# A block's opening: x loaded and turned first, half of the conditioning weights multiplied on TensorE

## The chip, the core and the metric

The kernel runs on one core of one Trainium2 chip. The metric is the device time of one execution in microseconds, and shorter is better. A core has five engines with queues of their own: TensorE (PE, matmuls and transposes; its weight loads are shown apart as PEld), VectorE (DVE), ScalarE (ACT), GpSimd (POOL) and SyncE (SP), which here only issues transfers. They wait for one another through semaphores. PE reads SBUF and writes PSUM, which has eight banks of 512 float32 per partition.

## The reference, cut to what matters

One decoder block: a conditioning vector `c` gives six vectors of 1024 numbers (`mod`), two of which scale and shift the normalised input before the big input projection.

```python
c_act = jax.nn.silu(c)                                        # (1, 1024)
mod = (c_act @ ada_w[l] + ada_b[l]).reshape(B, N_MOD, D)      # ada_w (1024, 6144)
shift1, scale1, gate1, shift2, scale2, gate2 = [...]
h = rms_norm(x, norm1_g[l]) * (1.0 + scale1) + shift1         # x (1024, 1024)
u = h @ w_in[l]
... gated linear attention, differential attention, merge, gate1
... rms_norm with shift2, scale2, a mixture of 32 experts, gate2
```

All inputs are float32. The block goes on from `u` through two attention branches and a mixture-of-experts layer. The change touches only the way to `h`, and the first use of `h`.

## The kernel before

All is written by hand for each engine, in one block per engine, and each block runs in its written order. There is no scheduler. The opening works on:

- `aw`, four buffers of 128 x 2048 for `ada_w`. Its 1024 rows are taken as 128 partitions x 8 rows (`KT` = 8), its 6144 columns as three groups of 2048. Group 0 holds shift1 and scale1. One load (`load_ada`, L332) brings one row per partition of one group, 1 MB. The loads of group 0 from j = 4 on wait until the buffer's former content has been used (`ada_done`).
- `ada(g, j)` on DVE (L1346): `acc[:, g, :] += aw[j] * c_act[j]` per partition, one instruction of 128 x 2048. After eight of them the sum over the partitions is still to be made. PE does it for group 0 with 16 matmuls against a column of ones (L632, moving size 1), whose results are 16 columns of PSUM bank 1: S1 and, after one more DVE instruction, A1 (`mod1_done`).
- `x_all`, 8 tiles of 128 tokens x 1024, in two loads of 2 MB (`load_x`, L348). ACT squares and sums each tile and takes a square root for each four; DVE takes the reciprocal and scales the four tiles (`normalise`, L1342). PE turns each tile with 8 transposes of 128 x 128 (L650) into two PSUM banks; a pair of banks serves every other tile.
- `hT`, the turned and modulated input, 128 x 8 x 1024. DVE reads the lower bank of a tile with four instructions `bank * A1 + S1` (`modulate`, L1343), ACT the upper bank with four (L1079). So no tile leaves PSUM before A1 and S1 are there.
- `project(n)` on PE: 8 token tiles x 8 matmuls of 128 x 512 for one 512-column section of `w_in`. Three sections run first, in a loop. `wring` holds two sections of weights, 2 MB each.

SP issues all loads in one row, and a wait there holds everything behind it. POOL fills constants and clears `acc` first (L478), which the load of `ada_b` into `acc` waits for.

Of the kernel before, what the change touches and what calls it, by code (L numbers as in the profile page):

```python
# [6 lines left out]
ALU = mybir.AluOpType  # L7
ACT = mybir.ActivationFunctionType
# [7 lines left out]
P = 128  # L16
T = 1024
D = 1024
NT = T // P
KT = D // P  # L20
# [11 lines left out]
LAMBDA_INIT = 0.8 - 0.6 * float(np.exp(-0.3 * 0))  # L32
# [49 lines left out]
PI = 3.14159  # L82

SEMS = """
c_ld early_ld small_ld fills_done consts_done mask0 ada_ld0 ada_ld1 ada_ld2 ada_ld3 ada_done
cact_1 rows_tr rows_cols mod1_ps mod1_done rope_step rope_arg rope_sin
lam_done
x_ld0 x_ld1 x_sq x_sd x_rs x_norm x_tr h_evd h_eva
w_ld proj_mm proj_free
# [17 lines left out]
N_SMALL = 15  # L107


def build(nc, io, out):  # L110

    with ExitStack() as ctx:
# [16 lines left out]
        def bank(b, n=1):  # L129
            return PS[:, b:b + n, :].rearrange("p b n -> p (b n)")  # L130
# [16 lines left out]
        onesf = sb("onesf", [P, P])  # L147
# [3 lines left out]
        gcols = sb("gcols", [P, 20])  # L151
# [6 lines left out]
        cact = sb("cact", [P, 4, KT])  # L158
        S1 = sb("S1", [P, KT])
        A1 = sb("A1", [P, KT])  # L160
# [137 lines left out]
        x_v = io["x"].rearrange("(t p) n -> t p n", p=P)  # L298
# [21 lines left out]
        def _(sp_):  # L320
            e = sp_
# [5 lines left out]

            def load_ada(g, j, dynamic):

                if dynamic or g * KT + j >= 4:  # L330
                    e.wait_ge(s["ada_done"], g * KT + j - 3)
                e.dma_start(aw[j % 4], ada_v[:, j, ds(g * 2048, 2048)]).then_inc(ada_ld[j % 4], 16)  # L332

            e.dma_start(cact[:, 0, :], io["c"].rearrange("(p j) -> p j", j=KT)).then_inc(s["c_ld"], 16)
            load_ada(0, 0, False)
            load_ada(0, 1, False)
            e.wait_ge(s["fills_done"], 1)
            small(rows[0:8, :], io["norm1_g"].rearrange("(k p) -> k p", p=P), "early_ld")
            for r, nm in ((16, "diff_q_g"), (17, "diff_k_g")):
# [7 lines left out]
            def load_x(g):  # L347
                e.dma_start(x_all[:, 4 * g:4 * g + 4, :],  # L348
                            x_v[4 * g:4 * g + 4].rearrange("t p n -> p t n")).then_inc(x_ld[g], 16)

            for j in range(2, KT - 2):
                load_ada(0, j, False)
            load_x(0)
            for j in range(KT - 2, KT):
                load_ada(0, j, False)
            load_x(1)
            e.dma_start(wring[:, 0], w_in_v[:, :, O_DQ:O_DQ + HW]).then_inc(s["w_ld"], 16)
            small(pos[:, :], io["positions"].rearrange("(t p) -> p t", p=P))
            small(gpre[:, 0, :], io["diff_q_g"][0:ROPE].partition_broadcast(P))
# [11 lines left out]
            assert n_small == {"early_ld": N_EARLY, "small_ld": N_SMALL}  # L371
            e.wait_ge(s["w_ld"], 16)
            e.dma_start(wring[:, 1], w_in_v[:, :, O_DK:O_DK + HW]).then_inc(s["w_ld"], 16)
            with e.Fori(1, 3) as g:
                for j in range(KT):
                    load_ada(g, j, True)
# [253 lines left out]
        def _(e):  # L630
            def mm(o, l, r, a=True, z=True):
                return nc.tensor.matmul(o, l, r, start=a, stop=z)  # L632
# [3 lines left out]
            e.wait_ge(s["consts_done"], 1)  # L636
            nc.tensor.transpose(bank(0)[:, 0:20], rows, ident[0:20, 0:20]).then_inc(s["rows_tr"], 1)

            e.wait_ge(s["ada_done"], KT)
            for j in range(2 * KT):  # L640
                last = mm(bank(1)[:, j:j + 1], acc[:, 0, j * P:(j + 1) * P], onesf[:, 0:1])
            last.then_inc(s["mod1_ps"], 1)


            for t in range(NT):
                e.wait_ge(s["x_norm"], t + 1)
# [2 lines left out]
                for k in range(KT):  # L649
                    last = nc.tensor.transpose(bank(4 + 2 * (t % 2) + k // 4)[:, (k % 4) * P:(k % 4 + 1) * P],  # L650
                                               x_all[:, t, k * P:(k + 1) * P], ident[:, :])
                last.then_inc(s["x_tr"], 1)
            e.wait_ge(s["small_ld"], 16 * N_SMALL)
            e.wait_ge(s["h_evd"], 2 + NT)
            e.wait_ge(s["h_eva"], 2 + NT)

            def project(n):

                e.wait_ge(s["w_ld"], 16 * (n + 1))
                for t in range(NT):  # L660
                    e.wait_ge(s["proj_free"], n * NT + t + 1)
# [5 lines left out]
            with e.Fori(0, 3) as n:  # L667
                project(n)


            e.wait_ge(s["ada_done"], 3 * KT)
# [5 lines left out]
            for b, (g, o) in enumerate(((1, 0), (1, 512), (2, 1024), (2, 1536))):  # L677
                last = mm(bank(4 + b), onesf[:, :], acc[:, g, o:o + 512])
# [4 lines left out]
            for t in range(NT):  # L683
# [370 lines left out]
            with e.If(n_ov > 0):  # L1054
                with e.Fori(0, n_ov) as j:
                    n = NB + j
# [20 lines left out]
        def _(e):  # L1077
            def act(o, i, f, **kw):
                return nc.scalar.activation(o, i, f, **kw)  # L1079
# [7 lines left out]
            act(cact[:, 1, :], cact[:, 0, :], ACT.Exp, scale=-1.0).then_inc(s["cact_1"], 1)  # L1087


            for g in range(2):  # L1090
                e.wait_ge(x_ld[g], 16)
                if g == 1:
                    e.wait_ge(s["x_sq"], 1)
                for j in range(4):
                    t = 4 * g + j
                    last = act(WK[:, 1024 * j:1024 * (j + 1)], x_all[:, t, :], ACT.Square, accum_out=xstat[:, 0, t:t + 1])
                last.then_inc(s["x_sq"], 1)
                e.wait_ge(s["x_sq"], g + 1)
                act(xstat[:, 1, 4 * g:4 * g + 4], xstat[:, 0, 4 * g:4 * g + 4], ACT.Sqrt, scale=1.0 / D,
                    bias=EPS).then_inc(s["x_sd"], 1)  # L1100
            e.wait_ge(s["mod1_done"], 1)
            for t in range(NT):
                e.wait_ge(s["x_tr"], t + 1)
                for k in range(4):
                    last = act(hT[:, 4 + k, t * P:(t + 1) * P], bank(5 + 2 * (t % 2))[:, k * P:(k + 1) * P], ACT.Identity,
                               scale=A1[:, 4 + k:5 + k], bias=S1[:, 4 + k:5 + k])
# [227 lines left out]
        def _(e):  # L1334
# [31 lines left out]

            e.wait_ge(s["rows_tr"], 1)
            v.tensor_copy(gcols[:, 0:19], bank(0)[:, 0:19])
            tsc(gcols[:, 19:20], bank(0)[:, 19:20], 1.0 - LAMBDA_INIT, ALU.mult).then_inc(s["rows_cols"], 1)


            def ada(g, j):
                n = g * KT + j
                e.wait_ge(ada_ld[j % 4], 16 * (2 * g + j // 4 + 1))
                e.wait_ge(s["ada_done"], n)
                stt(acc[:, g, :], aw[j % 4], cact[:, 3, j:j + 1], acc[:, g, :], ALU.mult, ALU.add).then_inc(s["ada_done"], 1)

            e.wait_ge(s["early_ld"], 16 * N_EARLY)
            e.wait_ge(s["fills_done"], 2)
            e.wait_ge(s["cact_1"], 4)  # L1380
            for j in range(KT):
                ada(0, j)


            def normalise(g):
                e.wait_ge(s["x_sd"], g + 1)
                v.reciprocal(xstat[:, 0, 4 * g:4 * g + 4], xstat[:, 1, 4 * g:4 * g + 4]).then_inc(s["x_rs"], 1)
# [4 lines left out]
            def modulate(t):  # L1392
                e.wait_ge(s["x_tr"], t + 1)
                for k in range(4):
                    last = tsc(hT[:, k, t * P:(t + 1) * P], bank(4 + 2 * (t % 2))[:, k * P:(k + 1) * P],
                               A1[:, k:k + 1], ALU.mult, S1[:, k:k + 1], ALU.add)
                last.then_inc(s["h_evd"], 1)

            normalise(0)
            e.wait_ge(s["mod1_ps"], 1)  # L1400
            e.wait_ge(s["rows_cols"], 1)
            v.tensor_copy(S1[:, :], bank(1)[:, 0:KT])
            stt(A1[:, :], bank(1)[:, KT:2 * KT], 1.0, gcols[:, 0:KT], ALU.add, ALU.mult).then_inc(s["mod1_done"], 1)
            e.wait_ge(s["mod1_done"], 1)
            modulate(0)
            modulate(1)
            normalise(1)
            for t in range(2, NT):
                modulate(t)


            e.wait_ge(s["small_ld"], 16 * N_SMALL)
# [482 lines left out]
```

## Time and profile before

| | us |
|---|---|
| median of three runs (1687.03 to 1690.07) | 1688.15 |
| the profiled execution | 1687.78 |
| its span, first to last instruction | 1686.0 |
| of it, start to the first matmul of the projection | 58.69 |
| from there to the second group of conditioning sums (L632, moving size 1) | 165.8 |

The profiled execution lies 0.37 us under the median. PE is busy for 93% of the span, but for a tenth of the first 42 us only. DVE has its densest stretch there, and the DMA queues as well. To read the opening, one looks at the chain of work that ended last from 0 to 59 us, then at the timeline of that stretch with all engines, and for PE's speed at its granted clock beside the time that equal instructions take. The time of an engine's group in the timeline is from its first start to its last end; a float32 matmul that is not a transpose shows as two records, so that 16 matmuls read x32.

### The profile page before, as it was taken

How to read it: one execution, taken by the hardware profiler on the slowest of the kernel's cores; microseconds unless marked ns; L12 is line 12 of the kernel's file. 1: busy time of each engine (PE TensorE's matmuls, PEld its weight loads, DVE VectorE, ACT ScalarE, POOL GpSimd, SP SyncE). 2: the span in 40 equal slices, each digit the busy share in tenths (PEclk: the TensorE clock that was granted, in tenths of full speed). 3: DMA queues.
4: the chain of work that ended last, by engine and by line, in shares of the span. 5: the costliest groups of instructions: out<-in, count | busy, mean ns of one | idle time of the engine just before them, and what ended most of it. 6: DMA issues, size and time to landing. Idle time of an engine off the chain costs nothing.

```text
span 1686.0 us, 20804 instructions
## 1 busy us (share of the span) xinstructions
PE 1561.2 (93%) x8215; PEld 698.1 (41%) x8215; DVE 483.5 (29%) x1012; ACT 341.3 (20%) x690; POOL 115.2 (7%) x142
## 2 busy tenths in 40 slices
PE   1899987999999999899999999959999999998996
PEld 1544453454545555444444445524333333232332
DVE  6840815232323223500111135553111111110111
ACT  2300323222223611300000123311111110110100
POOL 2000000000000000000000000010111111111101
PEclk9999989999999999899999999969999999999999
DMA  9860110001010000111115083168999999999994
GB/s 351 311 246 0 50 50 1 0 1 50 0 37 13 25 1 1 37 39 37 37 37 187 0 349 112 66 231 312 367 402 401 402 405 407 406 404 404 408 407 134
DMA packets 67371, 300.35 MB, mean 178 GB/s; under 512 B 9668, under 2 KB 34271, under 8 KB 51935
## 3 DMA queue, kind: packets, MB, share of 16 engines
q1 hardware_dynamic: 60400, 275.18, 41.3%
q0 software_dynamic: 6896, 24.12, 5.6%
q8 instruction: 53, 0.87, 0.2%
q14 instruction: 22, 0.18, 0.0%
HBM read 276.74 MB, written 22.54 MB: 178 GB/s over the span
## 4 chain that ended last, share of the span: by engine, by line
PE 83%; DMA 8%; DVE 4%; ACT 2%; issue 1%; POOL 1%; DVEq 0%; SPq 0%; ACTq 0%; POOLq 0%
PE PS L632 79%; DMA R<-in_expert_w 4%; DMA HT<-in_expert_w 2%; DVE R L1346 1%; PE PS L986 1%; PE PS L736 1%; ACT R L1079 1%; DVE att_mx L1504 1%; DMA R<-in_ada_w 1%; PE PS L1008 1%; DMA out_rows<-R 1%; PE PS L689 1%; DVE R L1338 1%; DVE R L1342 0%; PE PS L930 0%
## 5 line engine op out<-in xcount | busy, mean ns | idle before, releaser
L632 PE MATMUL PS<-R 128*32 128x512 f32 (+5 forms) x4040 | 731.7, 581 | 26.3 <-ACT R L1079 10.1
L632 PE MATMUL PS<-HT,R 128*32 128x512 f32 (+2 forms) x1376 | 409.3, 609 | 9.8 <-DMA R<-in_expert_w 7.4
L632 PEld LDWEIGHTS PS<-R 128*32 128x32 f32 (+4 forms) x4040 | 249.9, 127 | 388.4 <-issue 367.9
L632 PE MATMUL PS<-R,HT 128*128 x768 | 336.7, 596 | 2.7 <-ACT HT L1079 2.2
L632 PEld LDWEIGHTS PS<-HT,R 128*32 128x32 f32 (+1 forms) x1376 | 144.7, 142 | 194.7 <-issue 192.7
L632 PEld LDWEIGHTS PS<-R,HT 128*128 128x128 f32 x768 | 144.5, 191 | 176.3 <-issue 175.0
L1079 ACT ACTIVATE R<-PS 128x512 f32<-128x512 f32 (+4 forms) x148 | 87.7, 608 | 606.4 <-PE PS L632 455.1
L1338 DVE TENSOR_TENSOR R<-R,PS 128x512 f32<-128x512 f32 (+1 forms) x54 | 44.3, 842 | 541.6 <-PE PS L632 317.5
L597 POOL DMA_INDIRECT out_rows<-R x40 | 57.6, 1439 | 329.0 <-DVE R L1346 178.1
L1079 ACT ACTIVATE R<-PS,S,A 128x128 f32<-128x128 f32 x92 | 34.7, 457 | 193.3 <-PE PS L986 193.3
L632 PE MATMUL PS<-WK,R 128*32 128x512 f32 x416 | 70.6, 594 | 0.0
L1346 DVE SCALAR_TENSOR_TENSOR R<-PS,R,gate 128x1024 f32<-128x1024 f32 x23 | 29.5, 1284 | 139.0 <-PE PS L632 139.0
L1079 ACT ACT_TABLE_LOAD x30 | 38.5, 1283 | 137.6 <-PE PS L632 135.7
L1079 ACT ACTIVATE R<-PS,att_nm 128x128 f32<-128x128 f32 (+7 forms) x64 | 46.9, 737 | 88.7 <-DVE att_nm L1342 88.7
L1504 DVE TENSOR_REDUCE att_mx<-PS 128x2 f32<-128x256 f32 (+7 forms) x32 | 43.5, 1358 | 58.3 <-PE PS L632 58.3
L1346 DVE SCALAR_TENSOR_TENSOR R<-R,cact 128x2048 f32 (+1 forms) x24 | 56.4, 2351 | 5.2 <-DMA R<-in_ada_w 3.4
L632 PE MATMUL PS<-R,WK 128*128 (+3 forms) x376 | 45.6, 272 | 7.6 <-DVE WK L1338 5.0
L1079 ACT ACTIVATE WK<-PS 128x512 f32<-128x512 f32 (+9 forms) x40 | 25.4, 640 | 130.7 <-PE PS L736 114.6
L1342 DVE TENSOR_SCALAR R<-PS,att_rc 128x128 f32 x32 | 11.2, 351 | 140.6 <-PE PS L632 140.6
L1079 ACT ACTIVATE WK<-R 128x128 f32 (+4 forms) x56 | 34.3, 614 | 84.0 <-DVE R L1338 54.4
L632 PEld LDWEIGHTS PS<-R,WK 128*128 128x128 f32 (+2 forms) x376 | 38.6, 176 | 10.4 <-DVE WK L1338 5.2
L632 PE MATMUL PS<-onesf,R 128*128 128x1 f32 x64 | 14.7, 364 | 23.3 <-DVE R L1346 22.5
(221 smaller groups left out, 827.0 us busy)
## 6 DMA issues: line engine op xcount, KB each, us to landing
R<-in_expert_w SPq DMA_DIRECT2D x67, 2048.0 KB, 30.5
HT<-in_expert_w SPq DMA_DIRECT2D x20, 2048.0 KB, 24.0
R<-in_ada_w SPq DMA_DIRECT2D x24, 1024.0 KB, 5.6
WK<-in_expert_w SPq DMA_DIRECT2D x9, 2048.0 KB
R<-in_w_in SPq DMA_DIRECT2D x6, 2048.0 KB, 8.0
R<-in_w_in SPq DMA_DIRECT2D x16, 512.0 KB, 4.7
out_rows<-R SPq DMA_DIRECT2D x10, 512.0 KB, 3.7
R<-in_x SPq DMA_DIRECT2D x2, 2048.0 KB, 12.2
```

Source lines behind the costliest of these rows:

```text
L597: e.indirect_dma_start(out, bass.IndirectOffsetOnAxis(idx, 0), yb[u][p0:p1, :], None, compute_op=ALU.add).then_inc(s["sc_done"], 16)
L632: return nc.tensor.matmul(o, l, r, start=a, stop=z)
L689: last = nc.tensor.transpose(bank(4 + 2 * (t % 2) + h // NH)[:, (h % NH) * P:(h % NH + 1) * P], U[:, t, h * P:(h + 1) * P], ident[:, :])
L736: last = nc.tensor.transpose(bank(4 + j // 4)[:, (j % 4) * P:(j % 4 + 1) * P], attn[i % 2][:, j * P:(j + 1) * P], ident[:, :])
L986: last = nc.tensor.transpose(bank(j // 4)[:, (j % 4) * P:(j % 4 + 1) * P], xg[u][:, j * P:(j + 1) * P], ident[:, :])
L1008: last = nc.tensor.transpose(bank(4)[:, j * P:(j + 1) * P], hh[:, j * P:(j + 1) * P], ident[:, :])
L1079: return nc.scalar.activation(o, i, f, **kw)
L1338: return v.tensor_tensor(o, a, b, op)
L1342: return v.tensor_scalar(o, a, c1, None, op0)
L1346: return v.scalar_tensor_tensor(out=o, in0=a, scalar=c, in1=b, op0=op0, op1=op1)
L1504: v.tensor_reduce(att_mx[:, i % 2, :], score_v[:, :, 0:(i + 1) * P], AX.X, ALU.max).then_inc(s["max_ready"], 1)
```

## The change

It has three parts. (1) SP issues both loads of `x` directly after `c`, then the small early ones, then all eight loads of `ada_w`'s group 0 in a row. (2) Of these eight, the even ones go to DVE as before (`ada_first`), the odd ones to PE: `ada_mm(j)` multiplies 16 blocks of 128 x 128 of the buffer by column j of `c_act` and adds into the 16 columns of bank 1. They stand between the turned tiles, one behind each second tile, the last behind the sum of DVE's part. (3) A turned tile is copied out of PSUM unmodulated, by one instruction each on DVE and ACT, and `hT` is scaled and shifted in place afterwards, in two halves of 512 tokens: five of eight rows of blocks by DVE, three by ACT. The first section of the projection stands apart, and waits for the halves.

```diff
@@ SP
-                if dynamic or g * KT + j >= 4:
-                    e.wait_ge(s["ada_done"], g * KT + j - 3)
+                if dynamic:
+                    e.wait_ge(s["ada_done"], g * KT + j - KT + 1)
+                elif j >= 4:
+                    e.wait_ge((s["ada_done"], s["ada_mm"])[j % 2], j // 2 - 1)
...
-            load_ada(0, 0, False)
-            load_ada(0, 1, False)
+            load_x(0)
+            load_x(1)
...
-            for j in range(2, KT - 2):
+            for j in range(KT):
                 load_ada(0, j, False)
-            load_x(0)
-            for j in range(KT - 2, KT):
-                load_ada(0, j, False)
-            load_x(1)
...
+            e.wait_ge(s["ada_mm"], KT // 2)
             with e.Fori(1, 3) as g:
@@ PE
-            e.wait_ge(s["ada_done"], KT)
-            for j in range(2 * KT):
-                last = mm(bank(1)[:, j:j + 1], acc[:, 0, j * P:(j + 1) * P], onesf[:, 0:1])
-            last.then_inc(s["mod1_ps"], 1)
+            def ada_mm(j):
+                e.wait_ge(ada_ld[j % 4], 16 * (j // 4 + 1))
+                e.wait_ge(s["cact_1"], 4)
+                for f in range(2 * KT):
+                    last = mm(bank(1)[:, f:f + 1], aw[j % 4][:, f * P:(f + 1) * P], cact[:, 3, j:j + 1],
+                              j == 1 and f == 0, j == KT - 1 and f == 2 * KT - 1)
+                last.then_inc(s["ada_mm"], 1)
...
                 last.then_inc(s["x_tr"], 1)
-            e.wait_ge(s["small_ld"], 16 * N_SMALL)
-            e.wait_ge(s["h_evd"], 2 + NT)
-            e.wait_ge(s["h_eva"], 2 + NT)
+                if t % 2 == 1 and t < NT - 1:
+                    ada_mm(t)
+            e.wait_ge(s["ada_done"], KT // 2)
+            for f in range(2 * KT):
+                mm(bank(1)[:, f:f + 1], acc[:, 0, f * P:(f + 1) * P], onesf[:, 0:1], False, False)
+            ada_mm(KT - 1)
@@ ACT
+            def row_read(t):
+                e.wait_ge(s["x_tr"], t + 1)
+                act(hT[:, 4:KT, t * P:(t + 1) * P], bank(5 + 2 * (t % 2)).rearrange("p (k q) -> p k q", k=4),
+                    ACT.Copy).then_inc(s["h_eva"], 1)
...
+            for half in range(2):
+                c = slice(half * 512, (half + 1) * 512)
+                for k in range(5, KT):
+                    last = act(hT[:, k, c], hT[:, k, c], ACT.Identity, scale=A1[:, k:k + 1], bias=S1[:, k:k + 1])
                 last.then_inc(s["h_eva"], 1)
@@ DVE
-            for j in range(KT):
-                ada(0, j)
...
-            normalise(0)
-            e.wait_ge(s["mod1_ps"], 1)
...
+            for g in range(2):
+                normalise(g)
+                for t in range(4 * g, 4 * g + 4):
+                    column_read(t)
+                    if t % 2 == 1:
+                        ada_first(t - 1)
+            e.wait_ge(s["ada_mm"], KT // 2)
...
-            modulate(0)
-            modulate(1)
-            normalise(1)
-            for t in range(2, NT):
-                modulate(t)
+            e.wait_ge(s["h_eva"], 2 + NT)
+            for half in range(2):
+                c = slice(half * 512, (half + 1) * 512)
+                for k in range(5):
+                    last = tsc(hT[:, k, c], hT[:, k, c], A1[:, k:k + 1], ALU.mult, S1[:, k:k + 1], ALU.add)
+                last.then_inc(s["h_evd"], 1)
```

How PE's row opens, before. L637 turns the small gain rows, L632 is the sum of `acc` over the partitions, L650 turns x, L667 opens the loop of the projection:

```order
L637 MATMUL PS<-ident,R 128x20
L632 MATMUL PS<-onesf,R 128x1 x16
L650 MATMUL PS<-ident,R 128x128 x64
L667 UNCONDITIONAL_BRANCH
L667 ISA
```

And now, on PE again. `cact` marks the odd rows of `ada_w`, and x64 of 128x512 is the first section of the projection:

```order
L636 MATMUL PS<-ident,R 128x20
L651 MATMUL PS<-ident,R 128x128 x16
L631 MATMUL PS<-cact,R 128x1 x16
L651 MATMUL PS<-ident,R 128x128 x16
L631 MATMUL PS<-cact,R 128x1 x16
L651 MATMUL PS<-ident,R 128x128 x16
L631 MATMUL PS<-cact,R 128x1 x16
L651 MATMUL PS<-ident,R 128x128 x16
L631 MATMUL PS<-onesf,R 128x1 x16
L631 MATMUL PS<-cact,R 128x1 x16
L631 MATMUL PS<-R,HT 128x512 x64
```

The sum of `acc` moved behind the last transposes, and four blocks of 16 matmuls came in, three of them between pairs of tiles.

SP's row before, from behind the load of `c`. The order of issue is also the order in which the buffers fill:

```order
L332 DMA R<-in_ada_w 128x2048 x2
L326 DMA R<-in_norm_g 8x128
L326 DMA R<-in_diff_q_g 1x48 x2
L326 DMA R<-in_diff_k_g 1x48 x2
L326 DMA R<-in_gla_out_g 1x128
L326 DMA R<-in_diff_out_g 1x128
L326 DMA R<-in_ada_b 1x6144
L332 DMA R<-in_ada_w 128x2048 x4
L348 DMA R<-in_x 128x4x1024
L332 DMA R<-in_ada_w 128x2048 x2
L348 DMA R<-in_x 128x4x1024
L357 DMA R<-in_w_in 128x8x512
```

SP's row now:

```order
L336 DMA cact<-in_c 128x8
L338 DMA R<-in_x 128x4x1024 x2
L326 DMA R<-in_norm_g 8x128
L326 DMA R<-in_diff_q_g 1x48 x2
L326 DMA R<-in_diff_k_g 1x48 x2
L326 DMA R<-in_gla_out_g 1x128
L326 DMA R<-in_diff_out_g 1x128
L326 DMA R<-in_ada_b 1x6144
L334 DMA R<-in_ada_w 128x2048 x8
L355 DMA R<-in_w_in 128x8x512
```

Both loads of x moved ahead of all of `ada_w`. Of the eight loads in a row, the fifth and seventh wait for DVE, the sixth and eighth for PE.

DVE's row before, from the first `ada` to the end of the modulation:

```order
L1346 SCALAR_TENSOR_TENSOR R<-R,cact 128x2048 x8
L1387 RECIPROCAL sso<-sso 128x4
L1342 TENSOR_SCALAR R<-R,sso 128x1024 x4
L1402 COPY S<-PS 128x8
L1346 SCALAR_TENSOR_TENSOR A<-PS,gcols 128x8
L1343 TENSOR_SCALAR HT<-PS,A,S 128x128 x8
L1387 RECIPROCAL sso<-sso 128x4
L1342 TENSOR_SCALAR R<-R,sso 128x1024 x4
L1343 TENSOR_SCALAR HT<-PS,A,S 128x128 x24
```

DVE's row now, from the first `ada_first` on (ahead of it stand the first reciprocal, four scaled tiles and two copies):

```order
L1364 SCALAR_TENSOR_TENSOR R<-R,cact 128x2048
L1409 COPY HT<-PS 128x4x128 x2
L1364 SCALAR_TENSOR_TENSOR R<-R,cact 128x2048
L1402 RECIPROCAL sso<-sso 128x4
L1360 TENSOR_SCALAR R<-R,sso 128x1024 x4
L1409 COPY HT<-PS 128x4x128 x2
L1364 SCALAR_TENSOR_TENSOR R<-R,cact 128x2048
L1409 COPY HT<-PS 128x4x128 x2
L1364 SCALAR_TENSOR_TENSOR R<-R,cact 128x2048
L1426 COPY S<-PS 128x8
L1364 SCALAR_TENSOR_TENSOR A<-PS,gcols 128x8
L1361 TENSOR_SCALAR HT<-HT,A,S 128x512 x10
```

The eight big products became four, spread between the copies; the last stands behind the copy of the last tile, and the modulation moved behind all of it.

## Rows read from the trace of the kernel before

**Rows 1.** Page, part 2: busy tenths of PE and DMA in 40 slices of 42 us.

```profile
PE   1899987999999999899999999959999999998996
DMA  9860110001010000111115083168999999999994
```

**Rows 2.** Chain that ended last, in order of time: start us, us, what.

```profile
19.27 2.36 DVE R L1346
21.63 0.02 issue
21.65 10.07 DMA R<-in_ada_w
...
31.74 2.36 DVE R L1346
...
34.15 6.99 PE PS L632 x32
41.13 3.53 PE PS L650 x16
...
52.27 5.81 ACT HT L1079 x16
58.08 0.61 issue
58.69 101.55 PE PS L632 x236
```

**Rows 3.** Timeline, all engines: start us, us, engine, line, op, tiles, shape, count.

```profile
6.69 10.38 SPq L332 DMA_DIRECT2D R<-in_ada_w  x4
...
26.76 1.06 ACT L1079 ACTIVATE WK<-R 128x1024 f32<-128x1024 f32 x1 [23.72 <-DMA R<-in_x]
...
32.34 0.21 ACT L1079 ACTIVATE sso<-sso 128x4 f32<-128x4 f32 x1
...
34.01 0.17 DVE L1387 RECIPROCAL sso<-sso 128x4 f32<-128x4 f32 x1
...
34.22 2.74 DVE L1342 TENSOR_SCALAR R<-R,sso 128x1024 f32<-128x1024 f32 x4
```

**Rows 4.** Stretches of 2 us from the start: us, DVE busy, PEclk, DMA share, GB/s.

```profile
2.00:4.00 2.00, 0.93 (x1) 1.00 0.86 230
4.00:6.00 2.00, 2.00 (x1) 1.00 1.01 410
```

**Rows 5.** Timeline of PE alone, same columns as rows 3.

```profile
50.29 3.43 PE L650 MATMUL PS<-ident,R 128*128 128x128 f32 x16 [2.77 <-DVE HT L1343]
53.93 1.06 PE L650 MATMUL PS<-ident,R 128*128 128x128 f32 x8 [0.20 <-ACT HT L1079]
...
224.53 7.74 PE L632 MATMUL PS<-onesf,R 128*128 128x1 f32 x32 [0.78 <-ACT R L1079]
232.13 6.43 PE L632 MATMUL PS<-R,onesf 128*128 128x512 f32 x8
```

**Rows 6.** Stretches of 0.5 us: us, PE busy (records), granted clock, DMA share, GB/s.

```profile
36.00:36.50 0.50, 0.50 (x4) 1.00 1.00 377
...
53.00:53.50 0.50, 0.50 (x5) 0.64 1.03 401
...
226.50:227.00 0.50, 0.50 (x4) 1.00 1.04 406
227.00:227.50 0.50, 0.50 (x4) 0.94 1.09 426
...
230.00:230.50 0.50, 0.50 (x4) 0.50 1.04 381
...
237.50:238.00 0.50, 0.50 (x3) 0.82 0.00 0
```

**Rows 7.** Instructions grouped with their shapes, 0 to 75 us: count, busy, mean ns.

```profile
L1346 DVE SCALAR_TENSOR_TENSOR R<-R,cact 128x2048 f32<-128x2048 f32 x8 | 18.8, 2351 | 3.4 <-DMA R<-in_ada_w 2.7
...
L1342 DVE TENSOR_SCALAR R<-R,sso 128x1024 f32<-128x1024 f32 x8 | 5.5, 748 | 0.1
```

**Rows 8.** Timeline of DVE: reading one PSUM bank of 128 x 512.

```profile
242.48 0.75 DVE L1342 TENSOR_SCALAR R<-PS,gcols 128x512 f32<-128x512 f32 x1 [3.64 <-PE PS L689]
```

**Rows 9.** Loads of ada_w: issue to landing.

```profile
DMA to landing us min/median/max: 4.8/5.6/16.5
```

More of the change, by code:

```diff
@@ L84 @@
 SEMS = """
-c_ld early_ld small_ld fills_done consts_done mask0 ada_ld0 ada_ld1 ada_ld2 ada_ld3 ada_done
-cact_1 rows_tr rows_cols mod1_ps mod1_done rope_step rope_arg rope_sin
+c_ld early_ld small_ld fills_done consts_done mask0 ada_ld0 ada_ld1 ada_ld2 ada_ld3 ada_done ada_mm
+cact_1 rows_tr mod1_done rope_step rope_arg rope_sin
 lam_done
@@ L328, in load_ada, with load_x @@
             def load_ada(g, j, dynamic):
-                if dynamic or g * KT + j >= 4:
-                    e.wait_ge(s["ada_done"], g * KT + j - 3)
+                if dynamic:
+                    e.wait_ge(s["ada_done"], g * KT + j - KT + 1)
+                elif j >= 4:
+                    e.wait_ge((s["ada_done"], s["ada_mm"])[j % 2], j // 2 - 1)
                 e.dma_start(aw[j % 4], ada_v[:, j, ds(g * 2048, 2048)]).then_inc(ada_ld[j % 4], 16)
             e.dma_start(cact[:, 0, :], io["c"].rearrange("(p j) -> p j", j=KT)).then_inc(s["c_ld"], 16)
-            load_ada(0, 0, False)
-            load_ada(0, 1, False)
+            def load_x(g):
+                e.dma_start(x_all[:, 4 * g:4 * g + 4, :],
+                            x_v[4 * g:4 * g + 4].rearrange("t p n -> p t n")).then_inc(x_ld[g], 16)
+            load_x(0)
+            load_x(1)
             e.wait_ge(s["fills_done"], 1)
@@ L345, in _ @@
             small(acc[0:1, :, :], vec("ada_b").rearrange("a (g n) -> a g n", g=3), "early_ld")
-            def load_x(g):
-                e.dma_start(x_all[:, 4 * g:4 * g + 4, :],
-                            x_v[4 * g:4 * g + 4].rearrange("t p n -> p t n")).then_inc(x_ld[g], 16)
-            for j in range(2, KT - 2):
+            for j in range(KT):
                 load_ada(0, j, False)
-            load_x(0)
-            for j in range(KT - 2, KT):
-                load_ada(0, j, False)
-            load_x(1)
             e.dma_start(wring[:, 0], w_in_v[:, :, O_DQ:O_DQ + HW]).then_inc(s["w_ld"], 16)
@@ L652, in _, with project @@
                 last.then_inc(s["x_tr"], 1)
-            e.wait_ge(s["small_ld"], 16 * N_SMALL)
-            e.wait_ge(s["h_evd"], 2 + NT)
-            e.wait_ge(s["h_eva"], 2 + NT)
-            def project(n):
+                if t % 2 == 1 and t < NT - 1:
[4 more added lines that the diff above has]
+            ada_mm(KT - 1)
+            def project(n, first=False):
                 e.wait_ge(s["w_ld"], 16 * (n + 1))
                 for t in range(NT):
+                    if first and t % 4 == 0:
+                        e.wait_ge(s["h_evd"], 3 + NT + t // 4)
+                        e.wait_ge(s["h_eva"], 3 + NT + t // 4)
                     e.wait_ge(s["proj_free"], n * NT + t + 1)
@@ L665, in project @@
                     last.then_inc(s["proj_mm"], 1)
-            with e.Fori(0, 3) as n:
+            project(0, True)
+            e.wait_ge(s["small_ld"], 16 * N_SMALL)
+            with e.Fori(1, 3) as n:
                 project(n)
-            e.wait_ge(s["ada_done"], 3 * KT)
+            e.wait_ge(s["ada_done"], 5 * KT // 2)
             e.wait_ge(s["proj_free"], 4 + 3 * NT)
@@ L1100, in _ @@
                     bias=EPS).then_inc(s["x_sd"], 1)
+            for t in range(4):
+                row_read(t)
+            for t in range(4, NT):
+                row_read(t)
             e.wait_ge(s["mod1_done"], 1)
[L1102 to L1106, printed above, removed]
+            e.wait_ge(s["h_eva"], 2 + NT)
[3 more added lines that the diff above has]
+                    last = act(hT[:, k, c], hT[:, k, c], ACT.Identity, scale=A1[:, k:k + 1], bias=S1[:, k:k + 1])
                 last.then_inc(s["h_eva"], 1)
@@ L1368, in _ @@
             v.tensor_copy(gcols[:, 0:19], bank(0)[:, 0:19])
-            tsc(gcols[:, 19:20], bank(0)[:, 19:20], 1.0 - LAMBDA_INIT, ALU.mult).then_inc(s["rows_cols"], 1)
+            tsc(gcols[:, 19:20], bank(0)[:, 19:20], 1.0 - LAMBDA_INIT, ALU.mult).then_inc(s["rows_tr"], 1)
             def ada(g, j):
@@ L1374, in ada @@
                 e.wait_ge(ada_ld[j % 4], 16 * (2 * g + j // 4 + 1))
-                e.wait_ge(s["ada_done"], n)
+                e.wait_ge(s["ada_done"], n - KT // 2)
                 stt(acc[:, g, :], aw[j % 4], cact[:, 3, j:j + 1], acc[:, g, :], ALU.mult, ALU.add).then_inc(s["ada_done"], 1)
@@ L1390, in normalise, with column_read, ada_first @@
                     tsc(x_all[:, t, :], x_all[:, t, :], xstat[:, 0, t:t + 1], ALU.mult).then_inc(s["x_norm"], 1)
-            def modulate(t):
+            def column_read(t):
                 e.wait_ge(s["x_tr"], t + 1)
[L1394 to L1397, printed above, removed]
-            normalise(0)
-            e.wait_ge(s["mod1_ps"], 1)
-            e.wait_ge(s["rows_cols"], 1)
+                v.tensor_copy(hT[:, 0:4, t * P:(t + 1) * P],
+                              bank(4 + 2 * (t % 2)).rearrange("p (k q) -> p k q", k=4)).then_inc(s["h_evd"], 1)
+            def ada_first(j):
+                e.wait_ge(ada_ld[j % 4], 16 * (j // 4 + 1))
+                if j:
+                    e.wait_ge(s["ada_done"], j // 2)
+                stt(acc[:, 0, :], aw[j % 4], cact[:, 3, j:j + 1], acc[:, 0, :], ALU.mult, ALU.add).then_inc(s["ada_done"], 1)
+            for g in range(2):
[5 more added lines that the diff above has]
+            e.wait_ge(s["ada_mm"], KT // 2)
+            e.wait_ge(s["rows_tr"], 2)
             v.tensor_copy(S1[:, :], bank(1)[:, 0:KT])
@@ L1404, in _ @@
             e.wait_ge(s["mod1_done"], 1)
-            modulate(0)
-            modulate(1)
-            normalise(1)
-            for t in range(2, NT):
-                modulate(t)
+            e.wait_ge(s["h_eva"], 2 + NT)
+            for half in range(2):
[3 more added lines that the diff above has]
+                last.then_inc(s["h_evd"], 1)
             e.wait_ge(s["small_ld"], 16 * N_SMALL)
```

## The prediction

> **What bounds the kernel now.** I read three views. First the slices of the whole span [rows 1]: PE is full nearly everywhere, in the first slice it is busy for a tenth. What follows the opening hangs on PE's progress and not on absolute time, so a shift of the projection's first matmul should reach the end one for one. Its first 101.55 us are an unbroken row of PE work [rows 2], with nothing that could swallow a shift. The late stage with full DMA does not swallow it either: its transfers wait for routing results that PE's work makes.
>
> Second, the chain from 0 to 58.69 us [rows 2]. DVE's products of `ada_w`, 2.36 us each, run until 21.63; then DVE waits 10.07 us for the last two loads, which queue behind 2 MB of x. Then come 6.99 us of PE (16 matmuls of moving size 1), the transposes, the modulated reads of PSUM that free the banks, and at 58.69 the projection. PE has done 7 + 12 us of work by then and idled for the rest.
>
> Third, PE's speed. A transposed pair of tiles (16 transposes) takes 3.43 us at 50.29, and 8 transposes take 1.06 us at 53.93 [rows 5]: 0.214 against 0.13 us each. The granted clock between them rises from 0.50 to 1.00, inside 53.0 to 53.5 [rows 6]: from 1.2 to 2.4 GHz. The 16 matmuls of moving size 1 are 32 records in 6.84 us (34.15 to the next start at 40.99), 0.214 us each, four in each half microsecond. The clock column prints 1.00 there [rows 6], but the first 16 transposes behind them, 3.53 us [rows 2], have the price of the 0.50 stretch. So I take the engine as running at 1.2 GHz from 34 to 46, and the printed 1.00 as the absence of a record.
>
> **What the change removes.** From the path: the wait of 10.07 us, four of eight DVE products (4 x 2.36 = 9.4 us), and the order "sums first, tiles second". PE no longer needs A1 and S1 to empty a bank, so tiles can be turned as soon as x is there.
>
> **What it puts in their place, in order of time.**
>
> *x.* Its first load is issued near 1.3 us, first in the queue. The DMA moved 230 GB/s from 2 to 4 us and 410 from 4 to 6 [rows 4]; 2.1 MB are then through at 8.0, and I call it landed at 8.3. From landing to the end of the square root it takes 26.76 to 32.55, 5.8 us; reciprocal, start and first scaled tile take 0.9 more [rows 3]. First transpose: 8.3 + 5.8 + 0.9 = 15.0, with 0.3 for hand-offs 15.3. The small early loads now stand behind 4 MB of x and land near 13.5, just in time.
>
> *PE's row from there.* Eight tiles at 16 transposes per pair: 4 x 3.43 = 13.7 us. Four blocks of `ada_mm` and the sum over `acc`, all 16 matmuls with 128 x 128 weights and moving size 1: 5 x 6.84 = 34.2 us. That is where the change pays: DVE's 9.4 us became 27.4 us of PE, since a matmul of moving size 1 costs what its weight load costs.
>
> *Do others hold PE up?* Data: x's second half is through near 13, and four loads of 1 MB follow at 2.5 us each to 23.4; `ada_mm(1)` wants its load (18.3) at 18.8. The sixth load waits for `ada_mm(1)`, ends near 31 with 5.3 us to land [rows 9], and is wanted at 39. The eighth waits for `ada_mm(3)` at 36, lands near 42 and is wanted at 60. `w_in` is queued behind that at 36.5, lands near 45 with 3 MB ahead, and is wanted at 69; all the small loads queue behind it and are wanted later still. The second and third group of `ada_w` now start near 67 where they started at 48.9, DVE takes them from about 79 to 120, wanted at 237. So SP's new waits cost nothing. ACT reads its first bank after its second square root, near 19, before PE wants it. DVE: its second `normalise` ends near 35, the fifth tile is turned at 36. One wait is open: the sum over `acc` follows `ada_first(6)`, which follows the copy of the last tile: 0.75 [rows 8] + 2.35 [rows 7] + 0.1 = 3.2 us with PE idle.
>
> *The end of the opening.* 15.3 + 13.7 + 34.2 + 3.2 + 0.3 of hand-offs = 66.7. S1 and A1: 0.4 us as at 41. Then half 0 in place. No row shows 128 x 512 from SBUF to SBUF on DVE. Half of the 748 ns of a 128 x 1024 tile [rows 7] bounds it below, 0.37; the PSUM read of 0.75 [rows 8] bounds it above; I take 0.41, the nearer row being the SBUF one: 5 x 0.41 = 2.1, range 1.9 to 3.8. ACT's three lie beside that, half 1 beside the first four tiles of the projection. Projection at 66.7 + 0.4 + 2.1 + 0.1 = 69.3.
>
> *Its clock.* Before, the projection starts at full clock. Now it comes after 14 us of moving size 1, so at half clock, until the chip lets it rise. Rows show that 3.1 us after work began (50.29 to 53.35) and 5.5 us after (232.13 to 237.6) [rows 5, 6]. Half of that is lost: 1.5 to 2.7, I take 2.1.
>
> **The sum.** 69.3 + 2.1 - 58.7 = +12.7 us. Against the profiled execution 1687.78 + 12.7 = 1700.5, against the median 1700.9. I forecast 1700.5.
>
> **Two rules weighed.** The rows say that transposes alone lifted the clock: between 50.29 and 53.5 PE ran nothing else [rows 5, 6]. The Trainium skill, TensorE: Matmul & The Clock Gate, Part 4: PE-mode transpose, says that transposes do not count as busy work for the clock gate; by it no pair of tiles could lift the clock, and the first rival below would be void. The trace disagrees with it here.
>
> **Rivals.**
>
> *The clock rises in between (24%).* A pair of tiles at half clock lasts 3.43 us, and 3.1 us of transposes have been enough once [rows 5, 6]; behind matmuls of size 1 it took longer (from 41 to 46). If one of the four pairs lifts the clock, the block behind it runs fast until the clock falls, which took 2.9 us from 224.53 [rows 6]. The price of moving size 1 with adjacent weights at full clock is in no row. Bounds: 0.13 us, the transposes' price, and no gain at all, since the only such records at full clock, with strided weights, come four in a half microsecond at either level [rows 6]. So one rise is worth 0 to 3 us, and one to three of them worth 2 to 9: 1691.5 to 1698.5, middle 1695.
>
> *Full clock throughout, the other side (6%).* PE is busy almost without a gap from 15.3 on. If that keeps the clock at 2.4 GHz, a tile costs 1.06 and a block 32 x 0.13 = 4.2: PE is through with tiles 0 and 1 at 17.5, waits for data until 18.3, ends `ada_mm(3)` at 28.8, waits a little for DVE, ends tile 7 at 37.4, waits until 40.7, and ends at 49.1. With 2.6 for modulation the projection starts at 51.7, 7.0 earlier: 1680.8. It decides from the point where PE's 48 us of work shrink by more than 13 (the 10.6 to the old start, and the 2.1 of clock). Against it: seven microseconds of size 1 did not lift the clock at 34 to 41, and the same kind of work let it fall from 1.00 to 0.50 at 227.4 with PE never idle [rows 6]. The Trainium skill, the same page, section Why this matters for your kernels, advises to keep TensorE busy continuously to reach the full clock; by that rule this rival would be the forecast. The two stretches just named disagree with it.
>
> *Dearer reads and hand-offs (6%).* In-place products at the PSUM price add 1.7 us, the long clock rise 0.6, late small loads ahead of the first tile 1 to 2: 1703.5 to 1705.
>
> *No change within measurement (4%).* Two effects cancel: most pairs lift the clock and sizes of 1 are fast, near 1688.
>
> The forecast itself, 1698.5 to 1703.5, has 60%.
>
> **How the numbers follow.** A measurement of this kernel tells about 0.2%, 3.4 us, from no change: under 1684.8 is faster, over 1691.5 slower. Slower: 60 + 24 + 6 less a little at the edge = 0.88. Same: 0.06. Faster: 0.06. The range from 1691 to 1704 takes in the rises and most of the dear end and leaves out about 15%.
>
> **What would show it.** In the profile after: the first transpose at 15 (x first works), five groups of 32 records of moving size 1 with 6.8 us each (half of it: the clock rivals), one idle of PE of 3.2 us released by DVE's product, DVE's in-place group at 0.41 each, the first 128 x 512 matmul at 69 with a granted clock of 0.50 for 3 to 5.5 us, and an equal distance from there to the end. The forecast is wrong if the groups of moving size 1 take less than 5 us, or if the distance from the projection's start to the end changes by more than 3 us.

## The result, and the profile after

| | before | after |
|---|---|---|
| median | 1688.96 (5 runs) | 1700.95 (5 runs, 1695.66 to 1702.38) |
| ratio, 95% interval | | 1.0069 [1.0058, 1.0081] |
| profiled execution, span | 1687.78, 1686.0 | 1701.22, 1699.5 |
| first matmul of the projection | 58.69 | 70.95 |
| second group of conditioning sums | 224.53 | 238.18 |

The change makes the kernel 12 us slower, 0.7%. Nearly all of it lies in the opening. The slices of the page, 42 us each in busy tenths, beside [rows 1], already show it in the first one: PE is busy for six tenths where it was one, and DMA for seven where it was nine. DVE, whose row before opened with 6, is at four:

```profile
PE   6899998899999999899999999959999999998996
...
DVE  4470525332323223410000044563111111110111
...
DMA  7681110001010100021115073258999999999994
```

The chain of work that ended last, in order of time, beside [rows 2] (start us, us, what). The wait for `ada_w` is gone; from 17.16 to 68.17 every line is PE's own, but for some 3 us around the product of DVE at 51.95:

```profile
6.42 9.16 DMA R<-in_ada_b
...
17.16 3.67 PE PS L651 x16
20.83 6.68 PE PS L631 x32
27.52 3.52 PE PS L651 x16
31.03 6.62 PE PS L631 x32
37.65 3.52 PE PS L651 x16
41.17 6.62 PE PS L631 x32
47.78 3.53 PE PS L651 x16
...
51.95 2.35 DVE R L1364
54.30 0.04 issue
54.34 13.83 PE PS L631 x64
...
68.47 2.38 DVE HT L1361 x5
70.86 0.09 issue
70.95 89.21 PE PS L631 x204
```

The groups with their shapes, 0 to 90 us (count, busy us, mean ns, idle before), beside [rows 7]: the 128 records of the new blocks (four rows of `ada_w`, 16 matmuls each, two records a matmul) take 27.5 us, and the four products that DVE kept, as many as it gave away, 9.4:

```profile
L631 PE MATMUL PS<-cact,R 128*128 128x1 f32 x128 | 27.5, 349 | 0.0
...
L1364 DVE SCALAR_TENSOR_TENSOR R<-R,cact 128x2048 f32<-128x2048 f32 x4 | 9.4, 2343 | 0.0
...
L1361 DVE TENSOR_SCALAR HT<-HT,A,S 128x512 f32<-128x512 f32 x10 | 4.7, 544 | 0.0
L1088 ACT ACTIVATE HT<-HT,S,A 128x512 f32<-128x512 f32 x6 | 4.3, 801 | 16.5 <-DVE A L1364 16.5
```

### The profile page after: what moved, and what is told of

It is laid out like the page before. It is cut to its first block, busy times and chain, and to the rows that moved or that the text cites. A ratio compares the mean times of both kernels' runs of the same rounds, so it can differ in the third digit from the quotient of the medians.

```text
span 1699.5 us, 21007 instructions
## 1 busy us (share of the span) xinstructions
PE 1592.0 (94%) x8343; PEld 730.8 (43%) x8343; DVE 473.3 (28%) x994; ACT 337.9 (20%) x672; POOL 115.1 (7%) x142
## 4 chain that ended last, share of the span: by engine, by line
PE 82%; DMA 10%; DVE 4%; ACT 1%; issue 1%; POOL 0%; DVEq 0%; SPq 0%; ACTq 0%; POOLq 0%
PE PS L631 78%; DMA R<-in_expert_w 6%; DMA HT<-in_expert_w 2%; PE PS L745 1%; PE PS L995 1%; ACT R L1088 1%; DVE R L1364 1%; PE PS L651 1%; DVE att_mx L1529 1%; DMA out_rows<-R 1%; PE PS L698 1%; DVE R L1356 1%; DMA R<-in_ada_b 1%; PE PS L1017 0%; PE PS L939 0%
## 5 line engine op out<-in xcount | busy, mean ns | idle before, releaser
L631 PE MATMUL PS<-R,HT 128*128 (+1 forms) x768 | 338.1, 598 | 3.3 <-DVE HT L1361 2.8
L631 PE MATMUL PS<-WK,R 128*32 128x512 f32 x416 | 70.6, 594 | 0.0
L1364 DVE SCALAR_TENSOR_TENSOR R<-R,cact 128x2048 f32 (+1 forms) x20 | 47.0, 2350 | 4.9 <-DMA R<-in_ada_w 3.6
L1088 ACT ACTIVATE WK<-R 128x128 f32 (+4 forms) x56 | 34.2, 612 | 62.5 <-DVE R L1356 54.5
L586 POOL DMA_INDIRECT R<-xn_rows,R x23 | 22.8, 992 | 170.3 <-PE PS L995 90.7
```

What stands on the lines that cost most here:

```text
L586: e.indirect_dma_start(xg[u], None, xn_rows, bass.IndirectOffsetOnAxis(tab_tok[:, TURN[n]:TURN[n] + 1], 0)).then_inc(xg_ld[u], 16)
```

## The experiments

**First theory:** the four blocks of matmuls of moving size 1 lie on the path with their 27.5 us, at half clock. **Rivals:** the extra pass over `hT` or the early x is what costs; weight loads of this kind cost the same at either clock; the loads or DVE cover PE's row, so that its length does not matter. The kernel before was timed again beside each group of experiments: 1687.79 us (e1 to e4), 1688.14 (e5 to e7) and 1688.5 (e8, e9). Ratios below are against it.

**e1: all eight rows on DVE.** The second part of the change undone.

```diff
+                if dynamic or j >= 4:
+                    e.wait_ge(s["ada_done"], g * KT + j - 3)
...
-                if t % 2 == 1 and t < NT - 1:
-                    ada_mm(t)
-            e.wait_ge(s["ada_done"], KT // 2)
+            e.wait_ge(s["ada_done"], KT)
...
-            ada_mm(KT - 1)
...
                         ada_first(t - 1)
+                        ada_first(t)
```

> The changed kernel, but all eight rows of ada_w stay on DVE (two products behind each second tile); x first, plain copies and in-place modulation are kept. Theory (PE's four blocks of 16 matmuls of moving size 1, 6.83 us each, set the start of the projection): PE loses 27.4 us, DVE gains 4 x 2.35 = 9.4 us and becomes the bound; from 16.35 it has 5.7 of scaling, 5.5 of copies and 18.8 of products with some waits for PE, ending near 49; the sum on PE 6.9, modulation 2.8: projection near 58.5, time 1688 to 1690. Rival (the extra pass over hT, or the early start of x, is what costs): the projection stays at 66 or later and the time at 1697 or more.

Measured: projection at 57.67, 1688.18 us (1.0006 [0.9997, 1.0016] against before). So the whole loss goes when the four rows go back to DVE, and the rest of the change, x first, plain copies and the pass in place, comes out even with the kernel before. PE's timeline (start us, us, engine, line, op, idle before) now has the idle that the blocks had filled, and DVE is the one it waits for:

```profile
16.84 6.07 PE L640 MATMUL PS<-ident,R 128*128 128x128 f32 x32 [1.24 <-DVE R L1347]
32.80 6.60 PE L640 MATMUL PS<-ident,R 128*128 128x128 f32 x32 [9.90 <-DVE R L1347]
47.90 6.99 PE L628 MATMUL PS<-onesf,R 128*128 128x1 f32 x32 [8.49 <-DVE R L1351]
57.67 27.61 PE L628 MATMUL PS<-R,HT 128*128 128x512 f32 x58 [2.79 <-DVE HT L1348]
```

**e3: half of each block left out.**

```diff
-                for f in range(2 * KT):
+                for f in range(KT):
                     last = mm(bank(1)[:, f:f + 1], aw[j % 4][:, f * P:(f + 1) * P], cact[:, 3, j:j + 1],
```

> The changed kernel with 8 of the 16 matmuls of each of the four new blocks left out (the scale columns lack the odd rows of ada_w). Theory (the blocks lie on the path with their full length): 4 x 3.42 = 13.7 us less, less a little for loads that now come late: projection near 58, time near 1688. Rival (PE's row is covered by DVE or by the loads): the start moves by less than 5 us.

Measured: projection at 54.40, 1683.12 us in its one run: 16.6 us earlier than in the profile after, not 13.7. PE's timeline says where 3 more came from:

```profile
16.71 3.56 PE L651 MATMUL PS<-ident,R 128*128 128x128 f32 x16 [1.24 <-DVE R L1360]
20.11 1.92 PE L631 MATMUL PS<-cact,R 128*128 128x1 f32 x16
21.89 1.94 PE L651 MATMUL PS<-ident,R 128*128 128x128 f32 x16
25.04 1.95 PE L631 MATMUL PS<-cact,R 128*128 128x1 f32 x16 [1.20 <-DMA R<-in_ada_w]
```

Half a block took 1.92 and 1.95 us twice and 3.41 and 3.55 later, and the second pair of tiles took 1.94 where it had taken 3.65. Together that is some 4.7 us beyond the halving, against which stand new waits of 1.20 us for a load and 0.78 for DVE. But the edit did not bring the clock up: the first block is fast from its start at 20.11, and up to there this kernel does what the changed kernel does. That the first pair lifted the clock is the chance that e9 shows below. So the blocks lie on the path with their length, and about 3 of the 16.6 us are this one execution's.

**e2: the clock lifted ahead of the first tile.** Results of the four matmuls are unused.

```diff
             e.wait_ge(s["consts_done"], 1)
+            for _ in range(4):
+                mm(bank(2), onesf[:, :], zrow[:, 0:512])
+            e.wait_ge(s["early_ld"], 16 * N_EARLY)
```

> The changed kernel with four matmuls of 128 x 512 float32 on constants, results unused, put into PE's idle time before the first tile (11.3 to about 17), so that the first pair of tiles starts at full clock. Theory (a matmul of moving size 1 costs its weight load, and this goes with the clock): transposes of the first pair 0.13 us each, records of the first block behind it 0.11 to 0.13 us while the clock is up, 0.214 after it has fallen; the projection starts 2 to 6 us earlier, time 1695 to 1699. Rival (weight loads of 128 x 128 float32 cost 0.21 us at either level, as the strided ones do): the first block keeps 6.8 us, only the first pair saves 1.4 us, time 1699 to 1701.

Measured: projection at 63.12 in the profiled execution (1694.84), median 1698.01 of 4. The unedited kernel has the same median in e9 below (1697.97), so the times do not show that the lift at the start pays; what this run settles, it settles by its profile. Pairs of tiles and blocks in turn, PE's timeline:

```profile
18.60 1.97 PE L653 MATMUL PS<-ident,R 128*128 128x128 f32 x16 [1.24 <-DVE R L1362]
20.49 5.11 PE L631 MATMUL PS<-cact,R 128*128 128x1 f32 x32
25.46 3.65 PE L653 MATMUL PS<-ident,R 128*128 128x128 f32 x16
28.91 3.88 PE L631 MATMUL PS<-cact,R 128*128 128x1 f32 x32
```

Stretches of 1 us from 20 on (us, PE busy and records, granted clock, DMA share, GB/s):

```profile
21.00:22.00 1.00, 1.00 (x11) 1.00 1.02 426
22.00:23.00 1.00, 1.00 (x9) 0.79 1.02 426
23.00:24.00 1.00, 1.00 (x7) 0.50 0.38 156
...
28.00:29.00 1.00, 1.00 (x8) 0.50 0.95 246
29.00:30.00 1.00, 1.00 (x10) 0.79 0.94 377
30.00:31.00 1.00, 1.00 (x11) 1.00 0.85 352
```

With adjacent weights, a matmul of moving size 1 goes with the clock: a block takes 3.88 us mostly at 2.4 GHz and 6.83 at 1.2. The rival with one price at both levels falls. The clock also does what [rows 6] showed: it falls within such a block with PE never idle, and it rises again near the end of a pair of tiles or just behind it. The second, third and fourth pair each did so here, with rises at 29.4, 36.2 and 43.1 us.

**e9: the changed kernel again.** No edit.

> The changed kernel once more, without an edit, for a second profile and more times on another day. Theory (the opening runs at half clock in most executions, and in some a pair of tiles lifts the clock for a block): median 1699 to 1702, single executions down to 1695, and in the profile blocks of 6.8 us or one of 4 to 5. Rival (the start is fixed, and the spread comes from behind it): the projection starts within 0.5 us of 70.95.

Measured: median 1697.97 of 9 executions, 1691.72 to 1702.25, ratio 1.0045 [1.0029, 1.0062]; and in the profiled one the projection starts at 67.76, 3.2 us before that of the first profile. PE's timeline names the place:

```profile
30.76 6.83 PE L631 MATMUL PS<-cact,R 128*128 128x1 f32 x32
37.44 3.25 PE L651 MATMUL PS<-ident,R 128*128 128x128 f32 x16
40.53 4.06 PE L631 MATMUL PS<-cact,R 128*128 128x1 f32 x32
44.46 3.65 PE L651 MATMUL PS<-ident,R 128*128 128x128 f32 x16
```

The third pair of tiles (3.25 us) lifted the clock near its end, the third block took 4.06 in place of 6.83, and the clock was down again for the fourth pair. So it differs between executions of one program which blocks run fast. Both sets together, 14 executions, have their middle at 1698.65, 0.6% above the kernel before; the first set alone gave 0.7%, this one 0.45% by its ratio.

How often it happens can be read from the mean granted clock, which is known for every execution. The first profile of this kernel prints no level but 1.00 before 241 us, and its mean is 0.972; e9's prints 0.50 from 43.6, at the end of the fast third block, to 70.6, and its mean is 0.964. Of the 14 executions nine have a mean of 0.957 to 0.964 and took 1691.72 to 1698.82 us; the other five have 0.971 to 0.974 and took 1700.17 to 1702.38. Read so, the clock rose in the opening in nine of fourteen: in one of the first five and in eight of e9's nine. Only two of them have a profile, so this is a reading and not shown for the others.

**e8: operands swapped.** The vector is the stationary operand, a row of `ada_w` the moving one.

```diff
-                for f in range(2 * KT):
-                    last = mm(bank(1)[:, f:f + 1], aw[j % 4][:, f * P:(f + 1) * P], cact[:, 3, j:j + 1],
-                              j == 1 and f == 0, j == KT - 1 and f == 2 * KT - 1)
+                for b in range(4):
+                    last = mm(bank(2)[0:1, :], cact[:, 3, j:j + 1], aw[j % 4][:, 512 * b:512 * (b + 1)])
```

> The changed kernel with the operands of the four new blocks swapped: column j of c_act is the stationary operand (128 x 1) and a row of ada_w the moving one, four matmuls of 128 x 512 per block. Their results (a row in one partition) are not used, so the odd rows of ada_w are missing from shift and scale. Theory (the wide form costs its moving columns, 6.8 us a block at half clock and 3.4 at full, and lets the clock rise, which the form with moving size 1 does not): the clock is up from the second pair of tiles on, blocks take 3.4 us, pairs of tiles 2.0, the projection starts at 50 to 55, time 1682 to 1686. Rival (the chip grants the clock alike to both forms): blocks 6.8 us, projection at 70, 1700.

Measured: projection at 55.57, 1685.36 us, 0.9977 [0.9964, 0.9989]. PE's timeline:

```profile
20.56 3.76 PE L631 MATMUL PS<-R,cact 128*1 128x512 f32 x8
24.26 1.97 PE L650 MATMUL PS<-ident,R 128*128 128x128 f32 x16
26.16 3.60 PE L631 MATMUL PS<-R,cact 128*1 128x512 f32 x8
...
40.58 6.25 PE L631 MATMUL PS<-onesf,R 128*128 128x1 f32 x32 [3.04 <-DVE R L1363]
46.76 6.01 PE L631 MATMUL PS<-R,cact 128*1 128x512 f32 x8
55.57 34.73 PE L631 MATMUL PS<-R,HT 128*128 128x512 f32 x77 [2.79 <-DVE HT L1360]
```

The same products take 3.6 us a block and the tiles between them 1.97 a pair: the clock stayed up from the first block to 41.1. It fell there half a microsecond into the sum over `acc`, which kept the narrow form, but behind 3.04 us of idle too; which of the two brought it down no run here tells. The last block, mostly at half clock again, took 6.01 us, so at that level the forms do not differ much (6.83); what tells them apart is that three blocks and the tiles between them ran at full clock in this form. That its result, a row in one partition, must still be turned into columns is not in this time.

**e7: x first alone.** The first part of the change on the kernel before, with the sum on PE behind the second tile.

```diff
-            load_ada(0, 0, False)
-            load_ada(0, 1, False)
+            load_x(0)
+            load_x(1)
...
             normalise(0)
+            ada(0, 0)
+            normalise(1)
+            for j in range(1, KT):
+                ada(0, j)
```

> The kernel before with the first part of the change alone: both loads of x ahead, DVE scales all tiles between its products; banks are still emptied by modulating reads, so PE turns tiles 0 and 1 early and the six others after the sum. Theory (x first brings nothing while A1 and S1 stand between PE and its banks): sum at 41.1 to 48.1, then 12 to 13 us for the remaining tiles, projection near 61, 1689 to 1692. Rival (the early x is itself the gain): projection at 54 or earlier, 1684 or less.

Measured: sum at 41.06, projection at 61.96, 1690.27 us, 1.0014 [1.0004, 1.0025]. Early x alone brings nothing while the banks can only be emptied with A1 and S1: six tiles still come after the sum, and the sum is 6.9 us later than before (34.15). With plain copies and the pass in place the projection starts 4.3 us sooner (e1, 57.67), but that too only makes up for it: e1's time is that of the kernel before.

**e4: ACT alone reads the tiles.** e1 with the copies moved.

```diff
-                act(hT[:, 4:KT, t * P:(t + 1) * P], bank(5 + 2 * (t % 2)).rearrange("p (k q) -> p k q", k=4),
+                act(hT[:, :, t * P:(t + 1) * P], bank(4 + 2 * (t % 2), 2).rearrange("p (k q) -> p k q", k=KT),
                     ACT.Copy)
...
-            for g in range(2):
-                normalise(g)
-                for t in range(4 * g, 4 * g + 4):
-                    column_read(t)
-                    if t % 2 == 1:
-                        ada_first(t - 1)
-                        ada_first(t)
+            normalise(0)
+            ada_first(0)
+            normalise(1)
+            for j in range(1, KT):
+                ada_first(j)
```

> All eight rows on DVE, and ACT alone copies the turned tiles out of PSUM, both banks in one instruction of 128 x 1024 (about 1.1 us); DVE scales tiles 0 to 3, takes row 0, scales tiles 4 to 7, takes rows 1 to 7. Theory: DVE has 5.7 + 18.8 us from 16.35 and no wait for PE, so it ends at 41 if the loads keep ahead; sum on PE 6.9, modulation 2.8: projection near 50.7, 8 us earlier than before, 1.4 lost to a low clock at its start: 1681 to 1684. Rival (the loads bind: each buffer waits for DVE and takes 5 us to land): DVE ends near 46, projection near 56, 1686 to 1688.

Measured: projection at 50.89, 1681.57 us, 0.9959 [0.9945, 0.9973]: 0.4% under the kernel before, and the first complete variant here that gains. The loads keep ahead; DVE's products run in a row, here in its timeline:

```profile
21.32 2.74 DVE L1346 TENSOR_SCALAR R<-R,sso 128x1024 f32<-128x1024 f32 x4
23.98 17.08 DVE L1350 SCALAR_TENSOR_TENSOR R<-R,cact 128x2048 f32<-128x2048 f32 x7
```

**e5: one row given back to PE, in its idle time.** **e6: the rest of that idle time filled.**

```diff
+            e.wait_ge(ada_ld[0], 32)
+            e.wait_ge(s["cact_1"], 4)
+            for f in range(2 * KT):
+                last = mm(bank(1)[:, f:f + 1], aw[0][:, f * P:(f + 1) * P], cact[:, 3, 4:5], f == 0, False)
+            last.then_inc(s["ada_mm"], 1)
+            e.wait_ge(s["ada_done"], KT - 1)
...
-            for j in range(1, KT):
+            for j in (1, 2, 3, 5, 6, 7):
                 ada_first(j)
```

> The kernel in which ACT alone reads the turned tiles, with one of the eight rows (row 4) given back to PE, into the 13.6 us in which PE idles between the last tile (27.5) and the sum (41.1). Theory (a block on PE costs nothing while it fits into PE's idle time, and then saves DVE's 2.35 us): the sum starts at 38.7, the projection at 48.5, 2.4 us less: 1679. Rival (the loads or a late buffer take the gain): the sum starts at 41 or later, 1681 to 1682.

And e6 on top of it, with the results of the fillers unused:

```diff
             last.then_inc(s["ada_mm"], 1)
+            for _ in range(5):
+                mm(bank(2), onesf[:, :], zrow[:, 0:512])
             e.wait_ge(s["ada_done"], KT - 1)
             for f in range(2 * KT):
                 last = mm(bank(1)[:, f:f + 1], acc[:, 0, f * P:(f + 1) * P], onesf[:, 0:1], False, f == 2 * KT - 1)
             last.then_inc(s["ada_mm"], 1)
+            for _ in range(2):
+                mm(bank(2), onesf[:, :], zrow[:, 0:512])
```

> The same, and PE's idle time filled: five matmuls of 128 x 512 on constants ahead of the sum, two between the sum and the projection, results unused. Theory (moving size 1 goes with the clock, and the projection loses 1.4 us to a low clock at its start): the sum takes 3.7 to 5.5 us where it took 6.9, the projection starts at 45.5 to 47 and runs at full clock from its first matmul; 1674.5 to 1677. Rival (filling delays the real work as much as it saves): 1678 to 1680.

Measured: e5 projection at 49.67, 1679.28 us, 0.9947 [0.993, 0.9964]; e6 at 48.14, 1677.62 us, 0.9941 [0.992, 0.9962]. Half of e5's expected gain came: the sum starts at 39.88, 1.2 us and not 2.4 earlier, since the last two products now wait for their loads:

```profile
34.96 2.35 DVE L1358 SCALAR_TENSOR_TENSOR R<-R,cact 128x2048 f32<-128x2048 f32 x1 [1.34 <-DMA R<-in_ada_w]
37.48 2.35 DVE L1358 SCALAR_TENSOR_TENSOR R<-R,cact 128x2048 f32<-128x2048 f32 x1 [0.16 <-DMA R<-in_ada_w]
```

PE's own block cost 3.87 us there, since eight tiles in a row had lifted the clock. In e6 the sum took 4.61 us in place of 6.99, but the clock had fallen within it (at 42.8) and the two fillers behind it took 3.76 us. In the other profiles modulation takes 2.8 us after the sum, so they held the projection up by some 0.7 us, and gave it a better clock: from its start to the second group of sums it took 166.5 us against 168.5 in e5. The projection starts later than the 45.5 to 47 that I expected, it still runs its first 1.4 us at half clock, and the time lies between my two ranges. The intervals of e4, e5 and e6 overlap: what each of the two steps beyond e4 brings is seen in one profile each and not settled by the times.

## Why the prediction was right

Its terms for the profiled execution, by its own steps:

- **First transpose.** Predicted 15.3, measured 17.16: 1.9 too early. x was there at 9.53 and not 8.3. Half of that is the rate: from 2 to 4 us the DMA moved 101 GB/s where [rows 4], with other loads first, had 230, and the 0.26 MB between them take 0.6 us at the later 410. The rest is what lies between bytes moved and landing, for which I had put 0.3. That set the square root to 15.32 where 14.1 was forecast. The small early loads landed at 15.58, not 13.5, 9.16 us after their issue behind 4 MB of x, as the first line of the chain shows. So they and not the square root released the first tile: DVE took the reciprocal at 16.14, 0.8 us after the root was there. Of the 1.9 us, 1.2 are x and most of the rest is this.
- **PE's row.** Tiles: 3.5 us a pair in the chain against 3.43. Blocks: 6.6 to 6.9 against 6.84. The idle before the sum: 3.04 against 3.2. From first transpose to last sum 51.0 us against 51.1 forecast (13.7 + 34.2 + 3.2). This is the term that decides the sign, and e1 and e3 show it by taking it away.
- **No one else held PE up.** The chain has no load of `ada_w` and no other engine between 17.16 and 51.3; SP's new waits cost nothing here.
- **In place.** 5 in 2.38 us, 0.48 each; I took 0.41, inside bounds of 0.37 and 0.75. Projection at 70.95 against 69.3.
- **Its clock.** From the projection's start to the second group of sums: 167.23 us against 165.84 before, 1.4 lost, just under my range of 1.5 to 2.7. Its first ten records took 5.95 us, where the kernel before needed 101.55 for 236 [rows 2], 4.3 for ten. Other openings lost 1.5, 2.3 and 2.7 (e9: 167.4, e4: 168.1, e5: 168.5), and that is half of what their clock column prints at 0.50 behind the projection's start: 2.9, 4.6 and 5.4 us.
- **One for one to the end.** 13.65 us at the second group of sums, 13.5 over the span.

So the terms were short by 1.65 at the start of the projection and long by 0.7 in the clock, and the sum of 12.7 met 13.5 in the profiles and 12.0 in the medians.

That the medians came so close is in part luck. Of the rivals, **the clock rises in between** is real: e9's profile shows it in the changed kernel, and by the mean clocks it came in one of the first five executions and in eight of e9's nine. I gave it 24%, and the case without a rise 60%. Had the first set been like e9's, with its median of 1697.97, the change would have been 9.5 us and not 12: slower still, inside my range, but by that rival and not by my sum. Six of the 14 executions were under 1698.5, where I had drawn its edge. My bounds for the price at full clock, none to 0.13 us a record, were settled at the low end: 0.12 (3.73 us for 32 records in e6). **Full clock throughout** did not occur with this change in any profile; its condition, PE busy without a gap, was met from 17.16 to 51.3 and the clock did not stay up. The nearest to it is e8, in another form: with the clock up until 41.1 the projection starts at 55.57, where I had 51.7 for the clock up to the end. **Dearer hand-offs** came partly: late small loads cost 0.8 us ahead of the first tile.

One sign could not be seen: a granted clock of 0.50 at the projection's first matmul. The column prints 1.00 there in the first profile, and 0.50 in e9's.

## What to carry to other kernels

A product moved to an idle engine is free only while its price there fits into the idle time: here 2.35 us on DVE stood against 6.8 on PE. One row in PE's gap brought the projection's start forward by 1.2 us in its profile (e5), four on PE's path put it back by 12. For a vector times a matrix in float32 it is worth trying the vector on the stationary side, if the row that results can be used or turned cheaply; what the turning costs, no run here shows. Blocks of 128 x 128 with one moving column left TensorE at half clock for the 34 us of tiles and blocks in the first profile, in which it was never idle. What frees a buffer must be looked at with the move: early x gained nothing by itself (e7), came out even with plain copies shared by DVE and ACT (e1), and gained 6 us when ACT, the engine with slack, did all the copies (e4).

## What the runs showed of the hardware

- Matmuls of moving size 1 with adjacent float32 weights: 6.96 us for 32 records where the column prints 0.50 throughout (e9, from 58.00), 6.83 in its slow blocks before, 3.73 with the clock up throughout (e6, from 28.14), and 3.87 where it falls near the end (e5). With weights strided by 8 elements the same count takes 7.74 us in every profile, the first part of it at full clock [rows 5, 6].
- The clock falls to 0.50 during such matmuls with PE busy throughout: at 22.6 in e2 (0.79 from 22 to 23 us), 2.1 us after the block began. With wide matmuls and a single stationary column in place of three of these blocks it stayed up for 20 us (e8).
- The printed granted clock is 1.00 in the first profile of the changed kernel until 241 us, also where transposes took 0.22 us each (17 to 51). In all eleven profiles the first change that the column prints is a fall; rises ahead of it, as in e9 near 40 us, are not printed. Until then the column says nothing; the duration of a known instruction does.
- The changed kernel's executions spread over 10.5 us in e9 (1691.72 to 1702.25), those of before beside them over 8.8 (1685.62 to 1694.42). Two profiles of the same program differ by 3.2 us at the start of the projection. By the mean clocks above, executions with a rise in the opening make up the lower part of the spread; what moves the kernel before by as much, no run here tells.
